# Prompt scores inside the last sample round, compressed keys on a block diagonal, output weights in two loads, last down blocks by column range

## The reference

```
def trunk(x, pos, pool_prev, kv_past, win_prev, params):
    ...
        if layer < N_A_LAYERS:
            ...
            h = h + pool_mix(ext, n_prev, pool_w[layer], pool_scale[layer])
        else:
            if ctx is None:
                ctx = build_shared_kv(h, pos, kv_past, win_prev, kv_norm, w_kv, k_norm, ...)
            h = h + nsa_mix(xn, pos, ctx, w_qg[bi], q_norm[bi], w_o[bi])
        h = h + hmoe(rms_norm(h, norm_ffn[layer]), router_group[layer], router_expert[layer], ...)
```

```
    p_cmp = masked_softmax(s, ctx['cend'][None, :] <= qpos[:, None])
    o_cmp = jnp.einsum('bghtn,bgnd->bghtd', p_cmp.astype(ctx['cv'].dtype), ctx['cv'])
    ...
    return o.astype(xn.dtype).reshape(B, T, N_HEADS * HEAD_DIM) @ w_o
    ...
    for e in range(N_EXPERTS):
        gu = x2 @ w_gu[e]
        hdn = jax.nn.silu(gu[:, :D_EXPERT]) * gu[:, D_EXPERT:]
        y = y + comb[:, e:e + 1] * (hdn @ w_down[e]).astype(jnp.float32)
```

## Time and profile before

| | |
|---|---|
| median of 3 runs | 1054.05 us (1054.03 to 1057.02) |
| profiled execution, own time | 1058.02 us |
| its span | 1055.8 us |
| mean granted clock of TensorE in it | 0.947 |
| busy share: TensorE, DVE, ScalarE, GpSimd | 92%, 32%, 26%, 2% |
| HBM read | 279.55 MB |

### The profile page before, as it was taken

The page is one execution under the profiler, slowest core; times in us unless marked ns, Lnnn a source line. Parts: engine busy times, 40 slices in busy tenths (PEclk is TensorE's granted clock), DMA queues, the critical chain, the costliest instruction groups (busy, mean ns, idle before and its releaser), DMA issues. The chain is left out here.

```text
span 1055.8 us, 14599 instructions
## 1 busy us (share of the span) xinstructions
PE 974.8 (92%) x5576; PEld 528.3 (50%) x5577; DVE 341.8 (32%) x958; ACT 274.5 (26%) x594; POOL 22.2 (2%) x79
## 2 busy tenths in 40 slices
PE   3999999999998999879999999589986999999996
PEld 2876333343334444478767777456544333333333
DVE  2243022312223132810454452447526022312223
ACT  1131211121112111402556651346423211121111
POOL 0000000000000000210000000000000000000000
PEclk9999999999998999959999995789997999999998
DMA  9984999999998535388188460120019999999994
GB/s 327 368 326 161 370 409 408 409 409 409 409 409 296 199 130 215 121 198 277 50 259 278 134 210 22 54 112 2 1 63 396 409 409 409 409 409 409 409 410 189
DMA packets 94167, 287.56 MB, mean 272 GB/s; under 512 B 12224, under 2 KB 17728, under 8 KB 93063
## 3 DMA queue, kind: packets, MB, share of 16 engines
q1 hardware_dynamic: 93231, 282.92, 70.7%
q10 hardware_dynamic: 864, 3.67, 0.9%
HBM read 279.55 MB, written 15.50 MB: 279 GB/s over the span
## 5 line engine op out<-in xcount | busy, mean ns | idle before, releaser
L922 PE MATMUL bank<-arena 128*64 128x512 f32 x1024 | 241.0, 601 | 1.8 <-DMA arena<-in_w_gate_up 1.8
L922 PEld LDWEIGHTS bank<-arena 128*64 128x64 f32 x1024 | 65.7, 136 | 132.1 <-issue 126.1
L963 PE MATMUL bank<-arena,moe_hiddenT 128*64 128x512 f32 x512 | 113.8, 596 | 1.6 <-DMA arena<-in_w_down 1.6
L1129 DVE TENSOR_TENSOR residual<-bank,residual 128x512 f32<-128x512 f32 (+1 forms) x96 | 65.9, 688 | 59.2 <-PE bank L985 59.1
L1107 DVE TENSOR_TENSOR moe_hidden<-moe_silu,bank 128x256 f32<-128x256 f32 x32 | 13.5, 421 | 194.0 <-ACT moe_silu L1048 194.0
L985 PE MATMUL bank<-moe_down_parts,moe_scatter 128*128 128x512 f32 (+1 forms) x192 | 70.3, 459 | 4.5 <-DVE moe_down_parts L1120 4.5
L1048 ACT ACTIVATE moe_silu<-bank 128x256 f32<-128x256 f32 x32 | 12.3, 383 | 221.0 <-PE bank L922 220.9
L963 PEld LDWEIGHTS bank<-arena,moe_hiddenT 128*64 128x64 f32 x512 | 35.6, 137 | 66.0 <-issue 65.7
L273 PE MATMUL bank<-arena 128*128 128x256 f32 x192 | 48.1, 412 | 19.8 <-DMA arena<-in_pages_raw 17.0
L1120 DVE SCALAR_TENSOR_TENSOR moe_down_parts<-bank,moe_slot_weight,moe_down_parts 128x512 fp32r<-128x512 f32 x32 | 22.6, 747 | 108.5 <-ACT moe_down_parts L1066 108.5
L985 PEld LDWEIGHTS bank<-moe_down_parts,moe_scatter 128*128 128x128 f32 (+1 forms) x192 | 29.5, 181 | 54.0 <-issue 23.7
(11 more groups left out here) (321 smaller groups left out, 1153.8 us busy)
## 6 DMA issues: line engine op xcount, KB each, us to landing
arena<-in_w_gate_up SPq DMA_DIRECT2D x128, 1024.0 KB, 18.4
arena<-in_w_down SPq DMA_DIRECT2D x64, 1024.0 KB, 18.5
arena<-in_pages_raw SPq DMA_DIRECT2D x44, 256.0 KB, 3.9
arena<-in_pages_sel SPq DMA_DIRECT2D x32, 256.0 KB, 3.6
upper_b<-in_pages_sel SPq DMA_DIRECT2D x32, 256.0 KB, 3.5
out_new_win_sample<-in_state_win SPq DMA_DIRECT2D x1, 8064.0 KB
arena<-in_w_kv SPq DMA_DIRECT2D x3, 2048.0 KB, 21.1
arena<-in_cmp_w_rows SPq DMA_DIRECT2D x4, 1024.0 KB, 7.7
```

The source lines that it names most:

```text
L922: last = pe.matmul(ps[e % 2][g * CAP:(g + 1) * CAP, :], XS[:, k, x * CAP:(x + 1) * CAP], w[:, :, g, :], start=(k == 0), stop=(k == KD - 1))
L963: last = pe.matmul(ps[3 + half][x * CAP:(x + 1) * CAP, :], HT[:, x, c % 2, (c // 2) * CAP:(c // 2 + 1) * CAP], RW[:, (n + x) % RING, c % 2 ...
L1129: V.tensor_tensor(hv, scatter_bank(p, m)[0:rows, :], hv, ALU.add).then_inc(added, 1)
```

## The change

- Router: DVE copies the transposed logits earlier; the low parts of the three tiles come later, the second and third behind `build_gather`; the first gather waits for them one by one.
- `down` goes through pairs of chunks, and in each pair finishes column half 0 before half 1. A new semaphore says when half 0 of the last pair of chunks is done, and ScalarE's first half waits for that alone.
- The last pair of experts is scattered by half, three tiles each; the first three scatters wait for half 0 only, the stores for the fourth, fifth and sixth addition.
- The prompt's compressed keys are put on a block diagonal (`CKD`, a memset and two copies on DVE), so that one matmul with 128 contraction rows gives two heads: 16 matmuls of 32 columns, all in front of the first turn of round 8.
- Scores of the first two of the 16 pairs move into round 9, with DVE's `before` for both and ScalarE's exponentials for the first, in banks 0, 1, 2 and 7. They are methods of a class `PromptHeads`, which hold the code that `attend_prompt` had.
- The last sequence's turns alternate between banks 4 and 5.
- `w_o` is loaded in two transfers of 2 MiB, the first behind the samples' last loads, the second where the whole was loaded; the sample's projection waits for the second at its fifth piece. The output projection uses bank 3 in place of 7.

```diff
-    WO = 34384
+    WO = tuple(40528 + k * D for k in range(4)) + tuple(34384 + k * D for k in range(4))
...
+            dve.wait_ge(columns, 1)
+            V.tensor_copy(LT, ps[0][:, 0:TOK]).then_inc(lt_ready, 1)
             dve.wait_ge(rooted, 1)
             V.reciprocal(stat[:, 12:12 + NT], stat[:, 8:8 + NT]).then_inc(scale_in, 1)
             dve.wait_ge(scale_in, 1)
-            dve.wait_ge(columns, 1)
-            V.tensor_copy(LT, ps[0][:, 0:TOK]).then_inc(lt_ready, 1)
-            low_part(nc, dve, M, R, high, 0, low)
...
-            low_part(nc, dve, M, R, high, 1, low)
+            low_part(nc, dve, M, R, high, 0, low)
...
+        def step(p, m):
+
+            return divmod(m, 2) if p < PAIRS - 1 else (m % NT, m // NT)
...
-                    sp.wait_ge(added, NM * (PAIRS - 1) + 2 * i + 2)
+                    sp.wait_ge(added, NM * (PAIRS - 1) + NT + i + 1)
...
+                for m in range(NF // 2):
+                    n = UNITS * p + KD + 2 * m
+                    pe.wait_ge(unit_in[n % RING], landings(n))
+                    pe.wait_ge(unit_in[(n + 1) % RING], landings(n + 1))
                     for half in range(2):
-                        for x in range(2):
-                            last = pe.matmul(ps[3 + half][x * CAP:(x + 1) * CAP, :],
-                                             HT[:, x, c % 2, (c // 2) * CAP:(c // 2 + 1) * CAP],
-                                             RW[:, (n + x) % RING, c % 2, half * 512:(half + 1) * 512],
-                                             start=(c == 0), stop=(c == NF - 1))
-                            if half == 1 and c % 2:
-                                last.then_inc(used, 1)
+                        for c in range(2):
+                            for x in range(2):
+                                last = pe.matmul(ps[3 + half][x * CAP:(x + 1) * CAP, :],
+                                                 HT[:, x, c, m * CAP:(m + 1) * CAP],
+                                                 RW[:, (n + x) % RING, c, half * 512:(half + 1) * 512],
+                                                 start=(m + c == 0), stop=(m + c == NF // 2))
+                                if half == 1 and c == 1:
+                                    last.then_inc(used, 1)
+                        if half == 0 and m == NF // 2 - 1:
+                            last.then_inc(down_half, 1)
...
+                if p == PAIRS - 1 and m == NT:
+                    pe.wait_ge(yl, 2 * p + 2)
                 if m == 0:
-                    pe.wait_ge(yl, 2 * p + 2)
+                    pe.wait_ge(yl, 2 * p + (2 if p < PAIRS - 1 else 1))
...
-                act.wait_ge(used, UNITS * (p + 1))
+                act.wait_ge(down_half, p + 1)
                 act.wait_ge(ws, 2 * p + 2)
                 reach(act, scattered, NM * p)
                 for half in range(2):
+                    if half:
+                        act.wait_ge(used, UNITS * (p + 1))
...
+    rows = I["w_o"][0].rearrange("(k p) n -> p k n", p=P)[:, 4 * part:4 * part + 4, :]
+    sp.dma_start(view(M, Map.WO[4 * part], 4, D), rows).then_inc(M["wo_late" if part else "wo_in"], 16)
...
+    BANKS = (0, 1, 2, 7)
...
+    def scores(self, pe, u):
+        t, heads = self.pairs[u]
+        K = P * (t + 1)
+        for x, hd in enumerate(heads):
+            n = 2 * u + x
+            pp, j, h = self.rows_of(hd)
+            if n >= 4:
+                pe.wait_ge(self.masked, 2 * (n - 3))
+            pe.matmul(self.ps[self.BANKS[n % 4]][:, 0:2 * K], self.QR[pp, j, h, t * P:(t + 1) * P], self.KT[pp, :, j, 0:K],
+                      start=True, stop=True).then_inc(self.score, 1)
...
+            return 5 if b == NSEQ - 1 and q % 2 else 4
...
+            load_output_weights(sp, I, M, 0)
...
+                if b == NSEQ - 1 and q == 1:
+                    pe.wait_ge(pneg, 1)
+                elif b == NSEQ - 1 and q:
+                    pe.wait_ge(copied, 4 * b + q - 1)
...
+                pe.wait_ge(blocked, 2)
+                rows = ps[5][:, :].rearrange("p (t j r h c) -> p t j r h c", t=2, j=2, r=2, h=HPG)
                 for t in range(2):
-                    for hd in [x for x in range(NH) if x // HPG % 2 == par]:
-                        j, h, at = hd // HPG // 2, hd % HPG, (t * NH + hd) * CHUNK
-                        r = slice(par * HD, (par + 1) * HD)
-                        last = pe.matmul(ps[5][:, at:at + NCP], QN[r, j, h, t * P:(t + 1) * P], CKP[r, j, 0:NCP],
-                                         start=True, stop=True)
+                    for j in range(2):
+                        for h in range(HPG):
+                            last = pe.matmul(rows[:, t, j, :, h, :], QN[:, j, h, t * P:(t + 1) * P], CKD[:, j],
...
+                if i == ROUNDS[-1]:
+                    pe.wait_ge(masked, 4 * NSEQ - 2)
+                    prompt.scores(pe, 0)
+                    pe.wait_ge(expd, 4 * NSEQ - 3)
+                    prompt.scores(pe, 1)
                 if c:
                     compress(i - 1)
                 if i == NSEQ:
-                    prompt_scores(0)
+                    prompt_scores()
...
-                if i == NSEQ:
-                    prompt_scores(1)
...
+                    prompt.exps(act, 0)
...
+                st.add(V.memset(CKD, 0.0))
...
+                    V.tensor_copy(CKD[r, :, par, 0:NCP], CKP[r, :, 0:NCP]).then_inc(blocked, 1)
...
+                    prompt.before(dve, 0)
                     prompt_weights()
+                    prompt.before(dve, 1)
...
+            load_output_weights(sp, I, M, 1)
...
+                if k == KD // 2:
+                    pe.wait_ge(wo_late, 16)
...
-            scores(0)
-            scores(1)
             for u in range(NP + 1):
                 if u + 2 < NP:
-                    scores(u + 2)
+                    prompt.scores(pe, u + 2)
```

More of the change, by code:

```diff
@@ L1551, in samples @@
+def samples(nc, I, O, M, prompt):
     ps, OT = M["ps"], M["XT"]
@@ L2270, in project @@
             def project(tile, half, k, bank):
-                last = pe.matmul(ps[bank][:, :], OT[:, k, tile * P:(tile + 1) * P], WO[:, k, half * 512:(half + 1) * 512],
+                last = pe.matmul(ps[bank][:, :], OT[:, k, tile * P:(tile + 1) * P], WO[k][:, half * 512:(half + 1) * 512],
                                  start=(k == 0), stop=(k == KD - 1))
```

202 lines of the change are left out of this document (104 added, 98 removed).

## The result

The changed kernel takes 1030.06 us (median of 4 runs, 1027.85 to 1031.38), the kernel before 1055.47 in the same comparison (1054.03 to 1057.02): ratio 0.9757, 95% interval 0.9729 to 0.9785, 25.4 us less. The profiled execution after takes 1028.86, its span is 1026.8.

The account below looks back on a forecast made before the run. Layer 1's weight stream, starting when attention ends, and TensorE's timeline before that were taken as the bound. 1.9 + 6.6 + 2.0 + 9.0 + 1.6 = 21.1 off the 1054.05 median gave 1033.0 us, range 1026 to 1040.

Parts of the forecast that it names:

- round 8: Sample round 8: deleting one of two compressed-score blocks saves 6.94, less a 0.3 wait for ScalarE's copy: 6.6 us.
- layer 0's tail: End of layer 0: scattering by column half cuts TensorE's 2.26 wait to some 0.3; 1.9 us, bounds 0 and 2.3.
- The router's own stretch: Router edits in both layers: TensorE does not wait for the router, so 0; 2.6 us cost if both covers went.
- the second rival: Covers lost in round 9, both tails, output weights and stores: saving only 14.7, time 1039.4 us; chance 0.19.
- which moves along: Layer 0's end: the barrier, 2.47 in front of 340.07, was to shift with the tail's 1.9 us saving.
- The first rival: Clock stays up through rounds 8 and 9: they gain 13.0 and 4.6, saving 30.6, time 1023.5 us; chance 0.12.
- round 9: Sample round 9: added scores fit existing waits and alternating banks remove waits; 2.0 us, between 0.6 and 4.6.
- one sign set down for being wrong: Round 9: the fourth copy of turned weights or ScalarE's exponentials releasing a wait longer than 0.7 us.
- full-clock bound of 4.6: Round 9 at the full clock: turns end about 3 us sooner and the same chain gives 4.6 us.
- Start of prompt attention: Pair 3 turned 20.5 after the stage's start instead of 30.0; 9.5 less 0.5 for clock, 9.0 us; 6.7 to 10.
- Layer 1's tail: End of layer 1: the wait before the scatter goes, bunched stores cost some back; 1.6 us, bounds 0.8 and 2.2.
- The slower rival: Prompt attention, 700 to 782, granted the low clock: half the stage would cost 33, giving 1066 us; chance 0.02.

Follow-up runs that it names:

- by chunk: Changed kernel with down matmuls, ScalarE's wait and the last scatter in the old order, both layers; 24.6 us less than the kernel before, ratio 0.9769.
- one-bank kernel: Changed kernel with all turns of the last sequence in bank 4; 20.8 us less than the kernel before, ratio 0.9801.
- 128x15: Changed kernel with compressed scores as one block of 32 matmuls of 128 rows and 15 columns; 14.5 us less than the kernel before, ratio 0.9863.
- twice: Changed kernel with its block of 16 compressed-score matmuls computed two times in a row; 15.5 us less than the kernel before, ratio 0.9841.
- two blocks: Changed kernel with compressed scores as before: 32 matmuls of 64 rows, 15 columns, half behind the first turn; 14.7 us less than the kernel before, ratio 0.9853.
- 64x32: Changed kernel with 32 compressed-score matmuls of 64 rows, 28 of 32 columns, before the first turn; 12.7 us less than the kernel before, ratio 0.9875.
- exponentials: Changed kernel with ScalarE's four exponentials of prompt pair 0 behind the fourth copy of turned weights; 25.8 us less than the kernel before, ratio 0.9759.
- own stage: Changed kernel with the first two pairs' scores, maxima and exponentials back in prompt attention; 21.4 us less than the kernel before, ratio 0.9801.
- weights: Changed kernel with both pieces of the output weights loaded at the start of prompt attention; 21.8 us less than the kernel before, ratio 0.9803.
- spread: Changed kernel with exponentials behind the fourth copy and compressed scores in four groups between round 8's turns; 25.8 us less than the kernel before, ratio 0.9758.

## Why the prediction came out as it did

The time lay in the range, 2.9 below the forecast; the sum of 21.1 was 4.3 too small by the medians. The term that was most off is round 8: it was priced at the low clock, 6.6, and gave 12.1 in the profile, since the clock came back. That the range held is in part luck, since layer 0's tail, 1.9 too much, went the other way. The terms, read from the two profiles by where the later milestones moved (after against before):

- **Start of the program.** TensorE's first gather came at 95.50 instead of 96.50. The work in front of the router moved by that already, since the first matmuls on pages ran faster, so it is a difference of the executions. The router's own stretch did not change: 0 as forecast.
- **Layer 0's tail, 1.9.** At the barrier 2.4 was won (336.65 against 340.07, less the 1.0), of which the experiment by chunk gives 1.3 to the order and 1.1 to the clock. Of the wait's 2.26 DVE swallowed about 0.9, as the lower bound and the second rival had it: its second low half and then six additions end the layer. At the first sample matmul 0.6 in all was left, less than the 1.0 of the start. The step that failed is the barrier "which moves along": the projection stage behind it ends on a transfer, and this was not followed. No saving is seen at its end.
- **Round 8, 6.6.** 12.1 in this profile. The step that failed is to price the block and the turns behind it at the low clock, because a fall in a busy stretch had been seen there; how long the low clock would last was not asked. The price itself was right for that clock: in the execution of the one-bank kernel in which it stayed low, the block took 5.92 (5.84 forecast), and block to turns 30.37, which is 6.7 less than before. The first rival named what happened instead in round 8 (13.0), though not in round 9, where the clock fell. But it had the wrong reason, a gap filled and a denser matmul. The kernel before with the diagonal alone has no early matmuls and the same 24.94, and the runs with 128x15 and with the block twice show that the denser matmul alone does not hold the clock.
- **Round 9, 2.0.** From first turn to stage 14.90 became 11.66: 3.2. ScalarE's chain (copy, exponentials, copy) set it, as worked out. The turns ended 5.1 after the first of them, which was 9.4 before, and the wait for the fourth copy gave 2.1 of that back (2.62 for 0.51). So one sign set down for being wrong, a wait there of over 0.7, did appear, and the term still came out larger than forecast. Two readings in it were off: the timeline of before has three waits of 0.68 in front of the turns, and not four; and the full-clock bound of 4.6 is 3.6 by its own terms (0.6 and 3). The missing 1.0 is there in the rows: from the values to the next stage it took 4.93, and takes 3.97.
- **Start of prompt attention, 9.0.** 10.0: 30.01 became 20.05 at a full clock, so the half microsecond taken off for the clock was not needed. Not all of it is the moved work: with the old start and the clock at 1.00 throughout (the diagonal alone) pair 3 was turned 697.01 - 669.78 = 27.2 after the start, so about 7 is the change and 2.8 the low clock in the profile of before. The output weights did not wait. Their early half was worth 3.8 in the execution profiled without it, more than the 1.72 that the trace before showed: the shorter start meets them earlier (a wait of 2.13), and there the clock fell behind the wait.
- **Layer 1's stream.** First issue to last landing took 253.7 against 254.9. The ten experiments with the router edits lie between 253.6 and 255.0, and the one without has 255.0, so it need not be the edit. It was not forecast, and its cause is open.
- **Layer 1's tail, 1.6.** From the landing to the span's end 15.2 became 13.7: 1.5. That is the forecast's size; what the bunched stores cost in it was not measured by itself.

That is 1.0 + 0 + 12.1 + 3.2 + 10.0 + 1.1 + 1.5 = 28.9 of the spans' 29.0. Some 3.6 of that is a difference of the profiled executions from their medians; the 1.0 and the 1.1, which no edit accounts for, are of that size together.

By the timings, a part taken out by itself costs, against the 25.4 of the whole: the diagonal 10.7, the second bank for turns 4.6, the early scores 4.0, the early weights 3.6, the order of the down matmuls 0.8. These add up to 23.7. Each is good to some 4 to 5 us, so only the first two are clear of the noise. The router edits were not taken out by themselves.

How often the clock recovers is the term that a forecast needs here. From the block's first matmul to round 9's first turn:

| records in the block(s) | kernels | us |
|---|---|---|
| 64 | before, two blocks, 128x15, 64x32, twice | 37.1, 36.5, 37.2, 36.7, 37.5 |
| 32 in one block | changed, exponentials, own stage, by chunk, weights, diagonal alone | 24.9, 25.3, 26.6, 26.6, 25.2, 24.9 |
| 32 in one block | one bank | 30.4 |
| 4 times 8 | spread | 29.4 |

In these profiles the time went with the number of records and not with their shape; why one of seven stayed low with the same block is open.

Of the second rival's parts, the exponentials did stand in front of the last copy in round 9, and DVE took part of layer 0's tail; the weights were not waited for, and layer 1's tail came out as forecast. The slower rival's place, prompt attention, kept the full clock from its start on.

## What to carry to other kernels

Where a trace shows a stage at the low clock, price an edit in it twice: the deleted work at the rate shown, and also what stands behind it at the full rate, since a shorter run of narrow matmuls can give the clock back to what follows, as it did here in six profiles of seven. Follow a saving up to the next wait that ends on a transfer; in front of that it may be worth nothing, as layer 0's tail was here. A load that is just in time today can be late once the work in front of it shrinks: here a wait of 1.72 became one of 2.13. Read a difference of two profiles with the clock beside it, since part of it can be the clock's.

## What the runs showed of the hardware

- Fp32 matmuls with 128-column weights took the same time in shapes 128x15, 64x32 and 128x32: 0.20 us a record in blocks of 64 that ran nearly all at the low clock, and for 128x32 3.76 / 32 = 0.12 at the full one.
- TensorE's granted clock fell to the low level while it was busy without a pause, 1 to 4 us after a block of them began, in each of these shapes and in 64x15. In the changed kernel it had been busy for 5.8 us by then. After 64 such records it stayed low for 24 to 27 us, after 32 for 3 to 7 in four profiles, for 20 in one, and in two it did not fall until some 12 us after the block's start. The Trainium skill's page "TensorE: Matmul & The Clock Gate", section "HAM oscillation — how this bites in real kernels", puts the fall down to pauses of TensorE. These rows show falls without one, and a low clock that lasts through work without one (11.75 of 11.75 us busy at clock 0.50 in the block computed twice).
- A wait of 2.13 us for a transfer was followed by a projection of 3.56 instead of 1.94: the price of the wait was nearly doubled by the clock behind it. Behind a wait of 2.17 at the same place in another kernel the projection took 1.94.
